# Writing out the recurrent layer's rounds one by one on four engines

## The reference

```
def step(S, inp):
    r_t, w_t, k_t, v_t, kk_t, a_t = inp
    sa = einsum('bhij,bhj->bhi', S, -kk_t)
    S = S * w_t + sa (kk_t * a_t)^T + v_t k_t^T
    y = einsum('bhij,bhj->bhi', S, r_t)
```

## Time and profile before

| | |
|---|---|
| median of three runs | 2269.6 us |
| the profiled execution | 2273.93 us |
| its span | 2272.2 us |
| TensorE matmul busy | 2010.6 us, 88% |
| VectorE busy | 1049.2 us, 46% |
| ScalarE busy | 1011.8 us, 45% |
| GpSimd busy | 238.2 us, 10% |
| mean granted TensorE clock | 0.950 |

### The profile page before, as it was taken

One profiled execution on the slowest core, in us unless ns is written; L12 is line 12 of the kernel. 1 busy time (PEld: TensorE's weight loads), 2 busy tenths in 40 slices (PEclk: granted clock), 3 DMA queues, 4 the chain that ended last, 5 costly groups with the idle time before them and its releaser, 6 DMA issues.

```text
span 2272.2 us, 59485 instructions
## 1 busy us (share of the span) xinstructions
PE 2010.6 (88%) x24895; PEld 1710.4 (75%) x24895; DVE 1049.2 (46%) x1967; ACT 1011.8 (45%) x1735; POOL 238.2 (10%) x253
## 2 busy tenths in 40 slices
PE   6699989989898998999879789999899999989799
PEld 4687878878787887888769577777777777777477
DVE  2546556556556655665632443333333333333411
ACT  3444444444434444343431243555656464555621
POOL 0011111111111111111100021010101101010000
PEclk9899999999999999999969898999999999999799
DMA  5101000010100001010122211010001000010233
GB/s 189 47 2 44 5 26 26 10 39 7 42 7 26 24 7 44 7 42 7 54 84 85 94 31 29 19 37 19 28 28 28 28 19 29 18 37 9 75 111 111
DMA packets 103569, 89.44 MB, mean 39 GB/s; under 512 B 3973, under 2 KB 95736, under 8 KB 103112
## 3 DMA queue, kind: packets, MB, share of 16 engines
q1 hardware_dynamic: 100120, 68.50, 10.3%
q0 software_dynamic: 3040, 17.14, 2.0%
q10 hardware_dynamic: 208, 0.66, 0.1%
HBM read 64.96 MB, written 21.33 MB: 38 GB/s over the span
## 4 chain that ended last, share of the span: by engine, by line
PE 71%; DVE 11%; ACT 8%; issue 7%; DMA 2%; ACTq 0%; SPq 0%; DVEq 0%; POOLq 0%
PE ps L1661 6%; PE ps L1972 6%; PE ps L1973 6%; PE ps L1974 6%; PE ps L2049 5%; PE ps L1765 5%; PE ps L1662 4%; PE ps L1663 4%; PE ps L1597 2%; PE ps L1599 2%; PE ps L1598 2%; PE ps L1794 2%; PE ps L2007 2%; PE ps L1789 2%; PE ps L2033 2%
## 5 line engine op out<-in xcount | busy, mean ns | idle before, releaser
L1661 PE MATMUL ps<-xh,wh 128*128 128x258 f32 (+1 forms) x1024 | 323.7, 316 | 43.9 <-DVE arena L1275 22.9
L1662 PE MATMUL ps<-xh,wl 128*128 128x258 f32 (+1 forms) x1024 | 290.9, 284 | 0.0
L1663 PE MATMUL ps<-xl,wh 128*128 128x258 f32 (+1 forms) x1024 | 290.7, 284 | 0.0
L1972 PE MATMUL ps<-xh,wh 128*128 128x348 f32 x768 | 260.6, 339 | 19.7 <-ACT arena_b L1094 14.5
L1661 PEld LDWEIGHTS ps<-xh,wh 128*128 128x128 f32 x1024 | 193.2, 189 | 83.4 <-DVE arena L1275 28.4
L1973 PE MATMUL ps<-xh,wl 128*128 128x348 f32 x768 | 255.1, 332 | 0.0
L1974 PE MATMUL ps<-xl,wh 128*128 128x348 f32 x768 | 254.2, 331 | 0.0
L1546 DVE TENSOR_REDUCE arena_b<-ps 128x1 f32<-128x144 f32 (+4 forms) x224 | 106.8, 506 | 273.1 <-PE ps L2011 157.8
L2049 PE MATMUL ps<-arena_b 128*128 128x512 f32 (+4 forms) x448 | 186.7, 501 | 9.8 <-ACT arena_b L1118 9.8
L1662 PEld LDWEIGHTS ps<-xh,wl 128*128 128x128 f32 x1024 | 193.9, 189 | 0.9
L1663 PEld LDWEIGHTS ps<-xl,wh 128*128 128x128 f32 x1024 | 193.5, 189 | 0.0
(11 more groups left out here) (252 smaller groups left out, 4384.4 us busy)
## 6 DMA issues: line engine op xcount, KB each, us to landing
wr<-in_w_in SPq DMA_DIRECT2D x33, 512.0 KB, 4.3
xt_scr<-arena POOLq DMA_DIRECT2D x2, 4176.0 KB, 13.3
wr<-in_kv_w SPq DMA_DIRECT2D x16, 512.0 KB, 4.0
wr<-in_b_w_in SPq DMA_DIRECT2D x16, 512.0 KB, 4.1
arena<-xt_scr SPq DMA_DIRECT2D x8, 522.0 KB, 4.7
arena<-oa_scr SPq DMA_DIRECT2D x8, 520.0 KB, 3.6
arena<-in_x SPq DMA_DIRECT2D x8, 512.0 KB, 3.5
wr<-in_w_out SPq DMA_DIRECT2D x8, 512.0 KB, 4.6
```

The source lines that it names most:

```text
L1661: pe.matmul(bank, wh[:, j, k, :], xh[:, k, t], start=(k == 0), stop=False)
L1662: pe.matmul(bank, wl[:, j, k, :], xh[:, k, t], start=False, stop=False)
L1663: mm = pe.matmul(bank, wh[:, j, k, :], xl[:, k, t], start=False, stop=(k == KO - 1))
L1972: pe.matmul(bank[:, 0:SEG], wh[:, slot, k, :], xh[:, k, t], start=(k == 0), stop=False)
```

## The change

The loop over p becomes a Python loop that runs while the program is built, on all four engines. The instructions of the 24 rounds are thus all in the program, in the order in which the loop ran them, with constants where registers were.

```
--- before.py
+++ after.py
@@ -703,7 +703,7 @@
             round_pool(0, 2, round_order(2, True, True, True, True, True))
-            with pool.Fori(0, KO - 2) as p:
+            for p in range(KO - 2):
                 round_pool(p, 3, round_order(3, True, True, True, True, True))
                 for s_ in range(3):
                     round_pool(p + 1, s_, round_order(s_, True, True, True, True, s_ == 2))
@@ -975,7 +975,7 @@
-            with act.Fori(0, KO - 2) as p:
+            for p in range(KO - 2):
                 round_act_a(p, 3, round_order(3, True, True, True, True, True))
@@ -1439,7 +1439,7 @@
-            with dve.Fori(0, KO - 2) as p:
+            for p in range(KO - 2):
                 round_dve_a(p, 3, round_order(3, True, True, True, True, True))
@@ -1916,7 +1916,7 @@
-            with pe.Fori(0, KO - 2) as p:
+            for p in range(KO - 2):
                 round_pe_a(p, 3, round_order(3, True, True, True, True, True))
```

## The result

The changed kernel takes 2242.7 us (median of 4 runs, 2240.64 to 2244.97); before, measured beside it, takes 2267.76. The ratio is 0.9891, 95% interval 0.9874 to 0.9908. Measured once more with more runs of before, it was 2243.8 against 2266.59, ratio 0.9899 (0.9880 to 0.9917). The forecast was 2243.4. Its own profiled execution took 2242.74 us, with a span of 2241.1.

The account below looks back on a forecast made before the run. TensorE's taken branch, 3.4 us at each of five back edges, was taken to lie on the critical path. 25.48 us (five rounds) plus 0.74 (round (0,3)) made 26.2 off 2269.6: 2243.4 us; 8-in-10 range 2235 to 2256.

Parts of the forecast that it names:

- The place: Ahead of L1765, first step of round (p,3): TensorE's five taken back edges leave it idle 18.2 us, uncovered by other work.
- a sign of being wrong: Attention loop: its branches turning long because its code lies elsewhere would count against the forecast; TensorE's took 208 ns before.
- The granted clock: TensorE, rounds (0,-1) to (7,2): with no pause the clock stays at 1.00, against 0.91 to 0.95 in rounds behind a back edge.
- The control: Round (6,3), already written out behind the loop: its 32.87 us is what each round (0,3) to (5,3) becomes.
- The two parts of the 25.5 us: Rounds (1,3) to (5,3): 25.48 us go, 18.2 idle time and 7.3 (1.5 a round) left behind by the pause.
- Register work: Round (0,3), entered without a taken branch: loop-entry set-up and register-valued waits and addresses cost 0.74 us, which goes; bounds 0 to 0.74.
- The triples: Eighteen rounds (p+1,0) to (p+1,2): constants instead of registers change nothing, 0 us; at most 0.4 us lost, nothing gained.
- Code for the other engines: ScalarE, VectorE and GpSimd written out: some 3200 instructions, 27 new blocks, taken as 0 us with 0.6 us kept in range.
- The time: Whole kernel: 26.2 us off the median of 2269.6 gives 2243.4 us; this forecast was given 0.80.

Follow-up runs that it names:

- The pause made by hand: Changed kernel plus a seven-turn loop over one semaphore instruction on TensorE ahead of rounds (1,3) to (5,3); 2267.74 us in one run.
- The short pause: Changed kernel plus a two-turn loop over one semaphore instruction on TensorE ahead of rounds (1,3) to (5,3); 2245.15 us in one run.
- two pairs a turn: Kernel before, with TensorE's loop doing two head pairs in each of three turns, other loops kept; 2256.43 us against 2266.93, where 15.3 us less was expected.

## Why the prediction was right

*The place.* The pause ahead of L1765 was TensorE's taken branch. Writing out TensorE alone gives 24.2 of the 25.6 us of the stage, writing out the other three gives none. The attention loop's branches, named as a sign of being wrong, stayed at 0.21 us. The granted clock is 1.00 in rounds (0,0) to (7,2) as forecast; in (0,-1), for which I had written 1.00 too, it is 0.75, and was 0.74 before.

*The control.* Round (6,3) as the measure of the changed rounds was exact: 32.87 forecast, 32.84 to 32.87 measured, in seven places.

*The two parts of the 25.5 us.* I split them into 18.2 of idle time and 7.3, or 1.5 a round, that the pause leaves behind. The pause made by hand gives 4.90 - 3.52 = 1.4 a round, so the split stands as arithmetic. What it means is less simple. The short pause shows that 0.6 to 0.8 us of idle time disappear in waits that the round has anyway. And with the pause made by hand TensorE is busy 1.9 us longer in the mean of the five rounds (31.0 against 29.1), more than the 1.4 that are left. So those 1.4 are a net: what the clock costs, less what of the idle time is given back. I had read them as what the pause leaves behind alone. The sum, 4.9 to 5.1 us a round, is what was measured, and it holds for a pause of this length only.

*Register work.* Right for round (0,3), 0.8 us forecast as 0.74. I gave all of it to that round and none to the five others, where it is covered by the pause (37.97 us with and without it). This would have mattered had only the pauses gone: with TensorE alone written out, each of these rounds keeps 0.39 us, and with two pairs a turn 0.7 to 1.1 (33.53 to 33.99 over 32.85), as the missed 15.3 us show.

*The triples.* Forecast 0, with a bound of 0.4 us lost; measured 0.8 us lost (670.2 us against 669.4 for all seven). That is outside the bound. The step that failed, a small one, is to read from one written-out triple, whose three blocks happened to be cheap, that written-out code costs nothing. And it is not TensorE's code: in the stage of the kernels that leave the other engines their loops the triples last 669.1 to 669.4 us, with those written out 669.8 to 670.4. Of the loss 0.5 us are the two idle times ahead of ScalarE's L870. The second of them is in the seventh triple, whose code was constant in both kernels: only where in it the block falls has changed. The other 0.3 us were not placed.

*Code for the other engines.* Forecast 27 blocks at no price, with 0.6 us kept in the range; 19 came, and the triples lost 0.8. The estimate of 3200 instructions was too high too: a turn has 225 records on ScalarE, 282 on VectorE and 68 on GpSimd, 575 and not 640.

*The time.* 26.2 us off the median of 2269.6 gave 2243.4. The size was 25.6 in the stage, and 22.8 and 25.1 by the medians; that the number came out within 1 us owes something to the three runs of before that were known, whose median was 1.4 to 3.0 us above each of the later ones. That part is luck; the 26.2 us are the forecast, and they are 0.6 us off by the stage.

## What to carry to other kernels

Look for idle time with no releaser that comes exactly as often as a loop has back edges, and at the record of the branch itself; then compare a round inside the loop with the same round outside. On TensorE a loop is worth writing out when its body is longer than what is still at hand behind a branch; here the border lies between 1630 and 1980 instructions (matmuls, weight loads and the sequencer's own all count). The branch of a shorter one took 0.21 us a turn. The other engines' loops can stay if TensorE's goes: that gave 24.2 of the 25.6 us. Where a long loop must stay, put its back edge ahead of a wait that is there anyway, and behind work that TensorE still has to do: that alone gave 10 of 25 us here.

## What the runs showed of the hardware

- TensorE's taken branch takes 0.21 to 0.25 us with up to 1630 instructions in the body and 3.3 to 4.0 us from 1980 on, whether it is 1980 or some 10,000 (3.8 to 4.3 where it starts while matmuls are still running). Straight on, the same engine reads a block of 16.4 KB every 6.6 us (108 in 714 us) with no visible pause.
- A pause of TensorE of 0.81 to 0.91 us behind one of 1.27 us was enough in three of five cases for the granted clock to drop to 0.5 (1.2 instead of 2.4 GHz) for a time, at 1.1 to 1.6 us a drop; in the other two, with gaps of 0.86 and 0.81 behind 1.24 and 1.27, nothing fell.
- ScalarE's and VectorE's branches with bodies of 225 and 282 instructions (records of one turn in the trace, waits and register operations too) took 45 and 56 ns, and with 19 further blocks on their instruction queue the triples were 0.8 to 0.9 us longer in all, too little for the medians to show (ratio 1.0, 0.9991 to 1.0009). Of this 0.5 us are two idle times of 0.30 us on ScalarE, 0.65 us ahead of a block. What the other blocks did was not followed.
- Some 1100 semaphore increments in a row cost TensorE about (3434.55 - 2243) / 7 / 1100 = 0.15 us each.
